# A two-block transformer kernel: six small reorderings of splits, sums, banks and one transposition

## The reference, cut to what matters

```
first block:  u = rms_norm(x) * (1 + scale1) + shift1
              mix = mixer(u): projections of u; a gated short convolution; a state-space scan
                    (convolution, silu, dt = softplus(u @ w_dt + dt_bias), 32 heads,
                    group norm over 256 columns, gated by silu(z)); merged by sigmoids; @ w_o
              x = x + gate1 * mix
              u2 = rms_norm(x) * (1 + scale2) + shift2
              x = x + gate2 * (square(relu(u2 @ w_up)) @ w_down);   x = rms_norm(x) * final_norm
second block: u = modulated rms_norm(x) @ w_in: q and k normalized per head of 64, two kinds of attention
              x = x + g1 * (mixed @ w_out)
              x = x + g2 * ((silu(h2 @ w_gate) * (h2 @ w_up)) @ w_down)
```

## Time and profile before

| | before |
|---|---|
| median of three runs | 928.96 us |
| the three runs | 927.3, 928.96, 930.58 us |
| the profiled execution's own time | 927.08 us |
| its span | 925.3 us |
| PE busy | 890.7 us, 96% |
| DVE busy | 678.6 us, 73% |
| ACT busy | 543.0 us, 59% |
| POOL busy | 289.4 us, 31% |
| DMA | 203.02 MB, mean 219 GB/s |

### The profile page before, as it was taken

One profiled execution on the slowest core, in us unless ns is written; L12 is line 12 of the kernel. 1 busy time (PEld: TensorE's weight loads), 2 busy tenths in 40 slices (PEclk: granted clock), 3 DMA queues, 4 the chain that ended last, 5 costly groups with the idle time before them and its releaser, 6 DMA issues.

```text
span 925.3 us, 17831 instructions
## 1 busy us (share of the span) xinstructions
PE 890.7 (96%) x7390; PEld 858.2 (93%) x7390; DVE 678.6 (73%) x870; ACT 543.0 (59%) x840; POOL 289.4 (31%) x266
## 2 busy tenths in 40 slices
PE   5999999999999999998999999889999999999998
PEld 5899999999999999998999999878888999999998
DVE  5989997887776777768788767578995586755442
ACT  4477656457877864476656443467687674544431
POOL 5600003444377711176654111120003552212100
PEclk9999999999999999999999999999999999999999
DMA  9754555666686778854888887423233448755560
GB/s 366 292 212 175 183 205 206 229 234 248 233 301 222 262 262 291 290 184 141 306 300 286 300 319 282 162 92 134 95 137 108 166 147 325 269 208 180 174 225 24
DMA packets 36112, 203.02 MB, mean 219 GB/s; under 512 B 4928, under 2 KB 6080, under 8 KB 17216
## 3 DMA queue, kind: packets, MB, share of 16 engines
q1 hardware_dynamic: 36032, 201.89, 61.1%
HBM read 200.82 MB, written 1.05 MB: 218 GB/s over the span
## 4 chain that ended last, share of the span: by engine, by line
PE 63%; issue 14%; DVE 11%; POOL 5%; ACT 5%; DMA 1%; SPq 0%; ACTq 0%; POOLq 0%; DVEq 0%
PE acc L1140 55%; ACT w_hi L716 2%; DVE w_lo L1400 2%; DVE ada_w L1458 2%; DVE cv L1603 2%; POOL rt L613 1%; DMA ada_w<-in_ada_tiles 1%; PE m L1140 1%; PE m L1225 1%; POOL ysl L619 1%; DVE qk L1702 1%; POOL maps L660 1%; POOL ul L619 1%; PE acc L1105 1%; DVE maps L1696 1%
## 5 line engine op out<-in xcount | busy, mean ns | idle before, releaser
L1400 DVE TENSOR_TENSOR w_lo<-raw,w_hi 128x2048 fp32r<-128x2048 f32 x141 | 323.7, 2296 | 134.7 <-ACT w_hi L716 134.7
L1140 PE MATMUL acc<-uh,w_hi 128*128 128x256 f32 x1320 | 373.6, 283 | 4.2 <-DVE fr L1672 2.3
L1140 PE MATMUL acc<-ul,w_hi 128*128 128x256 f32 x1320 | 367.0, 278 | 0.0
L1140 PE MATMUL acc<-uh,w_lo 128*128 128x256 f32 x1320 | 366.9, 278 | 0.0
L716 ACT ACTIVATE w_hi<-raw 128x2048 fp32r<-128x2048 f32 x141 | 266.2, 1888 | 78.9 <-PE acc L1140 78.9
L1140 PEld LDWEIGHTS acc<-uh,w_hi 128*128 128x128 f32 x1320 | 249.5, 189 | 10.4 <-issue 5.4
L1140 PEld LDWEIGHTS acc<-ul,w_hi 128*128 128x128 f32 x1320 | 249.4, 189 | 0.4 <-issue 0.2
L1140 PEld LDWEIGHTS acc<-uh,w_lo 128*128 128x128 f32 x1320 | 249.3, 189 | 0.0
L1140 PE MATMUL acc<-hidh,w_hi 128*128 128x256 f32 x432 | 119.4, 276 | 0.0
L1140 PE MATMUL acc<-hidl,w_hi 128*128 128x256 f32 x432 | 119.2, 276 | 0.0
L1140 PE MATMUL acc<-hidh,w_lo 128*128 128x256 f32 x432 | 119.2, 276 | 0.0
(11 more groups left out here) (368 smaller groups left out, 1603.7 us busy)
## 6 DMA issues: line engine op xcount, KB each, us to landing
raw<-in_tiles SPq DMA_DIRECT2D x137, 1024.0 KB, 5.6
colw<-in_ada_cols SPq DMA_DIRECT2D x80, 512.0 KB, 5.3
ada_w<-in_ada_tiles SPq DMA_DIRECT2D x8, 1024.0 KB, 17.0
raw<-in_rest SPq DMA_DIRECT2D x4, 768.0 KB, 4.6
cact<-in_c_rows SPq DMA_DIRECT2D x2, 512.0 KB, 4.2
xT<-in_x SPq DMA_DIRECT2D x1, 1024.0 KB, 7.3
first_w<-in_tiles SPq DMA_DIRECT2D x1, 1024.0 KB, 17.1
out<-xT SPq DMA_DIRECT2D x8, 128.0 KB, 3.8
```

Of the source, the lines that this page charges most:

```text
L1140: ins = pe.matmul(o, l, r, start=(s.k == 0 and i == 0 and not j), stop=(s.last and i == s.kts - 1 and j == 2))
L1400: dve.tensor_tensor(lo, raw_of(n), hi.bitcast(F32), ALU.subtract).then_inc(S("lo_ready"), 1)
```

## The change

It moves work in the queues and changes one bank; no arithmetic is added or removed.

1. dt's transposition by PE goes from behind the second half of step 4 to behind the first half of step 5, and DVE's addition of the bias from the first half of step 5 to the second, where it stands behind the three taps.
2. `z_sum` stands behind the second half of its step in place of the first.
3. In the third up step DVE makes the low weights of step n + 2 after it has drained both banks, in place of before.
4. `x_sum_ahead` goes from within the last half of the last `dn` step to behind it; ACT's table load goes one step earlier.
5. The second head norm's sum (jq = 2) is taken in M4 in place of M0.
6. The sum of the norm ahead of the gate steps (`x_sum(4)`) stands ahead of chunk 7 of the first gate step in place of chunk 3. That of the up steps stays ahead of chunk 3.

```
+    SUM_AT = (3, 7)
...
+        def Q_BANK(jq):
+
+            return ("M4", M4) if jq == 2 else ("M0", M0)
...
-                if (s.kind, s.j) in (("wo", 2), ("dn", 3), ("o2", 2)) and s.last:
+                if n == D_LAST - 1 or (s.kind, s.j) in (("wo", 2), ("o2", 2)) and s.last:
                     log_exp_table()
...
-                        inverse_root(qr, M0[:, :], HD, "qroot")
+                        inverse_root(qr, Q_BANK(jq)[1][:, :], HD, "qroot")
...
-                        if n == D_LAST and nb == NB - 1 and i == KB - 2:
-                            x_sum_ahead()
                         product_part(n, nb, i)
...
-                        if n in LATE and (m, b, i) == (n, 0, 3):
+                        if n in LATE and (m, b, i) == (n, 0, SUM_AT[LATE[n] // 2]):
                             x_sum(LATE_NORM[LATE[n] // 2])
...
-                    if nb == 0 and 2 <= n - Z0 < 10:
+                    if nb == 1 and 2 <= n - Z0 < 10:
                         z_sum(n - Z0 - 2)
...
-                        take("M0")
-                        pe.wait_ge(S("qsq"), NB * (jq + 1))
                         jq += 1
-                        pe.matmul(M0[:, :], blk64[:, :], sq[:, 2:4, :].rearrange("p a b -> p (a b)"), start=True, stop=True)\
+                        name, bank = Q_BANK(jq)
+                        take(name)
+                        pe.wait_ge(S("qsq"), NB * jq)
+                        pe.matmul(bank[:, :], blk64[:, :], sq[:, 2:4, :].rearrange("p a b -> p (a b)"), start=True, stop=True)\
                           .then_inc(S("qsum_done"), 1)
-                        free["M0"] = ("qsum_read", jq)
+                        free[name] = ("qsum_read", jq)
...
-                    if n == 4 and nb == 1:
+                    if n == 5 and nb == 0:
                         pe.wait_ge(S("dt_t"), 1)
...
                 if s.kind == "dn" and s.j == 3 and s.last:
+                    x_sum_ahead()
                     x_sum(2)
                     keep_busy(7)
...
-                if n + 2 < NS and not split_late(n) and s.kind != "xbc" and not adds_tokens(n) and n not in LATE and n != D_LAST:
+                if n + 2 < NS and not split_late(n) and s.kind != "xbc" and not adds_tokens(n) and n not in LATE and n not in (D_LAST, U0 + 2):
                     split_lo(n + 2)
...
-                        if nb == 0 and n == 5:
+                        if nb == 1 and n == 5:
                             dve.wait_ge(S("dt_tr"), 1)
...
+                        if n == U0 + 2 and nb == NB - 1:
+                            split_lo(n + 2)
...
-                        ins = dve.scalar_tensor_tensor(qt, M0[:, :], HD * EPS, qr, ALU.add, ALU.mult)
+                        ins = dve.scalar_tensor_tensor(qt, Q_BANK(jq)[1][:, :], HD * EPS, qr, ALU.add, ALU.mult)
```

## The result

The changed kernel takes **923.39 us** (median of 7 runs, 922.72 to 925.83), the kernel before on the same chip 929.21 (7 runs, 927.3 to 932.23). The ratio is 0.9936, 95% interval 0.9918 to 0.9954: 0.64% faster. The profiled execution took 922.89 us with a span of 920.9, against 927.08 and 925.3 before. The forecast was 923.2 and its sum -4.9 us; the two profiled executions are 4.2 apart, the two medians 5.8.

A forecast was written before the change was run, and what follows sets the result against it. TensorE, busy nearly the whole span, was read as the bound through its waits. Terms summed to -4.9 us: 922.2 against the profiled execution, 924.1 against the median; it took 923.2, range 919.8 to 926.9.

The forecast's parts named there:

- dt, +1.5: Steps 5 to 8: bias addition behind three taps makes VectorE, without slack, 1.5 us later; bounds 0 and 1.7.
- Group norm, -2.8: Sums after the second bank: all three TensorE waits covered, 2.8 us saved; bounds -2.0 and -3.4.
- Third up step, -1.8: Third up step: first bank drained ahead of the split, saving 1.8 us; bounds -1.2 and -2.2.
- Middle norm, -2.0: Last down step: six products run before the sums, deciding sum 2.0 us earlier; bounds -1.6 and -2.1.
- Head norm, 0: Second head norm's own bank: scores still need both norms applied, so 0 us; bounds 0 and -0.9.
- Gate step, +0.2: First gate step: the 2.5 us wait splits, GpSimd's low parts still awaited, +0.2 us; bounds +0.4 and -1.0.
- every wait is gained: Rival, all six places: the full 12.6 us is saved, 916; half-way (-8 or better) counts; chance 0.06.
- the waits come back behind: Rival, group norm and up step: GpSimd's drains and the late split cost it back, 0 to -2.8, 927.3; chance 0.17.
- The clock: Rival, slower: new waits bring 1.2 GHz stretches of 1.7 us each; five more make it slower, 932; chance 0.04.

The follow-up runs named there:

- The filler: Kernel after with dt's bias early, last down step's split behind the last drain, and unread matmuls in two TensorE waits: 0.9899, 919.87 us; repeated 0.9897, 919.71 us.

## Why the prediction was right

The mechanism held: where a wait was removed, the queue of the engine met next fixed what was left of it. The terms of the group norm and the up step were somewhat too large, for one reason: TensorE's lead met a bank that VectorE still had to drain.

- **dt, +1.5:** +1.47 alone, +1.62 after, by the named cause: the bias's addition behind three taps of 1.51, all of which undoing it gives back. One detail was off: the wait in step 8 of about 2 us came in pieces (alone, 2.0 at three banks, 0.7 at most, where before had 0.9 at two, and 0.6 for `dta`).
- **Group norm, -2.8:** 3.12 at the place, of which 2.54 was left at 336.08 (2.24 alone). The prediction said that a lead of 2.8 us costs no new wait in the steps behind, by a walk through VectorE's queue. That was wrong by 0.6: VectorE's bank at L1656 takes it back, as a wait of 0.3 where the products run fast and hidden under them where they run slow. The low weights, which the walk was about, are not what TensorE met. The larger gain at the place covered for it.
- **Third up step, -1.8:** 1.94 at the place, 1.49 kept. The lateness of the split didn't heal as cheaply as I reckoned: with its successor right behind it and GpSimd beside both, two took 5.05, and the drain behind them came late enough to make TensorE wait 0.3. Both figures lie inside the bounds of 1.2 and 2.2.
- **Middle norm, -2.0:** 1.99, alone and after.
- **Head norm, 0:** the scores are fixed by the two engines that apply the norms. The waits were forecast at 1.5 and then 0.9 to 2.5; they were 1.66 and 2.50.
- **Gate step, +0.2:** +0.22 and +0.24, with two waits of 1.0 forecast and 0.94 and 1.22 found. These sizes are hardly above what pace alone does there.

The terms together: +1.62, -0.21 (drift from 89.66 to 257.47), -2.54, -1.49, -1.99, +0.38 and -0.26 (pace and gate step), and 0.04 at places between, make -4.45 against -4.9 in the forecast.

That the median came within 0.2 us of 923.2 is partly luck. The forecast added to its sum 0.9 us for fewer stretches at 1.2 GHz, as the mean of two ways to reckon it. There were fewer: 1.6 per timed run on average, against 2.2 in the 67 runs of before in the experiments, by the count explained below. But the runs of one kernel lie 3 to 5 us apart, and the interval of the ratio allows a gain of 4.3 to 7.6 us.

**The rivals.** That every wait is gained (12.6 us) is out: 1.66 + 2.50 and 0.94 + 1.22 stand in place of 2.4 and 2.5. That the waits come back behind is true by 0.6 of 3.1 for the group norm and by 0.45 of 1.94 for the up step, and for neither in full. The clock is a real mechanism and was given the right price: forecast 1.7 a stretch, found 1.57, 1.58 and 1.9 where TensorE waits for nobody, and nothing where it does. It just doesn't add up to a loss: in the profiled execution a new stretch came with an old one gone, and the timed runs have fewer than before. It does set how far runs lie apart.

**What whole runs can't show.** The six ratios alone add to -1.03%, 9.6 us, while the kernel after has -0.64%. The traces of the same six say +1.47, -2.24, -1.49, -1.99, 0 and +0.24, that is -4.0. Each of the ratios is uncertain by 0.11 to 0.17%, 1.0 to 1.6 us, and runs with different numbers of stretches at 1.2 GHz are mixed in each. The record lets them be told apart. In all 14 profiled executions the mean granted clock of the run follows the number of stretches: 1.000 for none, 0.998 for one, 0.996 for two, 0.993 for four. Of the 67 timed runs of before in the experiments, 14 stand at 0.998 with a median of 927.8 us, 26 at 0.996 with 929.4 and 26 at 0.994 with 930.2. Fitted over all timed runs with one price for a stretch (1.2 us, an estimate, since one costs 0 to 1.9 by its place), the six parts come to +1.4, -3.0, -1.8, -3.0, +0.2 and +0.4, each give or take 0.6 to 0.9: -5.7 in all, give or take 2.1. Most of what was too much in the six ratios is the clock; only the middle norm stays 1.0 above its trace, and why is open. A term of 1.5 us is read off the trace, not off six timings.

## What to carry to other kernels

Price a removed wait by what arrives next: redo the queue of the engine that the waiting one meets behind it, and where that engine has no pause (taps after dt, norms before scores) the wait only moves or the order costs you. When an in-order engine gets a short operation from another's result, putting it behind longer work costs the length of that work for everyone behind, 1.5 us here for an addition of 0.22. A lead lasts only as far as the next bank that another engine drains: of 3.1 us won at the group norm, 2.2 to 2.5 were left 20 us on. And once a wait for a GpSimd sum is short, look at what VectorE streams beside it: moving one split out of the way halved the additions (2.94 to 1.43 us) and was worth 1.0 us beside the 2.0 of the moved sum.

## What the hardware did that I had not expected

- **Two paces of the same matmul at full clock.** Products of 256 columns follow each other at about 113.3 ns or at about 117.7, each for long stretches, and not in the same places in every execution: from 315 to 336 us of before the products are slow with dt's edit alone and fast before, in the same code. Such a part costs 0.9 us (+1.77 to +2.63 between 314.32 and 336.08). Of the times from one product's start to the next, 1259 lie between 116 and 119 ns before, 1251 after and 1690 with dt alone. Changes of pace came with a wait or another kind of matmul; what chooses between the two is open.
- **A stretch at 1.2 GHz comes behind a long wait, but not behind each.** Behind 60 us and ahead of the end, the 14 profiled executions have 20 stretches. Of these, 19 begin within 2.4 us of the end of a wait of TensorE of 1.7 to 2.5 us (the other is the one at 81.4, behind two waits of 0.7); 15 of the 34 waits of that size have none. Around 620 us six executions have one (619.3 to 621.3), and the work may be within 2 us of before or 5 to 6 us ahead of it there: in the first case the wait at the head norm's sum ends just ahead of it, in the second the wait ahead of the scores. The two waits of 2.3 and 2.5 us that the change removes were such places: in the kernels that have them, 3 of 6 executions have a stretch behind the first (439.4 to 443.0) and 2 of 6 one behind the second (744.2 and 746.8); in the kernels without them none of 8 has one. What decides whether a stretch follows a wait is open. One cost 0 or about 1.6 us around 620, by what lay under it. The filler cut the waits of 2.5 and 1.8 to 0.8 and 0.3 to 0.5, and the stretches went with them.
